# Merging the convolution branch last in layer 0 of a two-block network, with most of its taps behind attention

## The reference, cut to what matters

```python
def conv_module(val, glu, gate, dw_w, dw_b, ln_g, ln_b, w_o):
    u = val * jax.nn.sigmoid(glu)
    u = lax.conv_general_dilated(u, dw_w[:, None, :], ..., feature_group_count=D_CONV) + dw_b   # 31 taps
    u = jax.nn.silu(layer_norm_2(u, ln_g, ln_b)) * jax.nn.silu(gate)
    return u @ w_o
...
def merge(p, ya, yb, yc):
    return (sigmoid(p[13]) * ya + sigmoid(p[14]) * yb + sigmoid(p[15]) * yc) @ w_out
xs = xs + gate_x * merge(px, ya_x, yb_x, yc_x)
if need_ctx:                    # layer 0 only
    cs = cs + gate_c * merge(pc, ya_c, yb_c, yc_c)
```

## Time and profile before

| | us |
|---|---|
| median of 3 executions | 1399.64 (1398.94 to 1400.97) |
| profiled execution, own time | 1403.85 |
| its span, first to last instruction | 1402.5 |
| TensorE busy in the span | 1318.3 (94%) |
| VectorE, ScalarE, GpSimd busy | 865.4, 594.3, 278.2 |
| mean granted TensorE clock, share of full | 0.964 |

### The profile page before, as it was taken

One profiled execution on the slowest core, in us unless ns is written; L12 is line 12 of the kernel. 1 busy time (PEld: TensorE's weight loads), 2 busy tenths in 40 slices (PEclk: granted clock), 3 DMA queues, 4 the chain that ended last, 5 costly groups with the idle time before them and its releaser, 6 DMA issues.

```text
span 1402.5 us, 18894 instructions
## 1 busy us (share of the span) xinstructions
PE 1318.3 (94%) x7490; PEld 1041.7 (74%) x7490; DVE 865.4 (62%) x1484; ACT 594.3 (42%) x983; POOL 278.2 (20%) x217
## 2 busy tenths in 40 slices
PE   7999887989979899997999999999999998799998
PEld 5777776867767777775777877777888876578876
DVE  4694646784578643488997532324586678845553
ACT  3444442444474455222434532223463563346442
POOL 0200102210022322237100011311252142201112
PEclk9999988999989999998999999999999998989998
DMA  7571566275253411111111122222553333123451
GB/s 250 213 256 57 181 224 210 91 254 182 91 181 111 158 61 52 55 61 61 62 59 45 61 90 90 91 90 90 156 175 95 106 106 93 57 77 121 147 177 66
DMA packets 49192, 168.46 MB, mean 120 GB/s; under 512 B 5862, under 2 KB 7078, under 8 KB 48848
## 3 DMA queue, kind: packets, MB, share of 16 engines
q1 hardware_dynamic: 49104, 167.26, 35.9%
HBM read 166.19 MB, written 1.05 MB: 119 GB/s over the span
## 4 chain that ended last, share of the span: by engine, by line
PE 72%; DVE 11%; issue 11%; POOL 4%; ACT 1%; DMA 1%; SPq 0%; POOLq 0%; DVEq 0%; ACTq 0%
PE bank L1467 15%; PE bank L1468 15%; PE bank L1469 15%; PE bank L1386 4%; PE bank L1780 3%; PE bank L1485 3%; DVE conv_val L2523 3%; DVE w_lo L2210 2%; PE bank L1486 2%; PE bank L1487 2%; PE bank L1755 1%; PE bank L1547 1%; PE bank L1510 1%; PE bank L1716 1%; PE bank L1463 1%
## 5 line engine op out<-in xcount | busy, mean ns | idle before, releaser
L1467 PE MATMUL bank<-w_hi,x_hi 128*128 128x512 f32 (+4 forms) x1120 | 466.0, 416 | 13.2 <-DVE w_lo L2210 8.0
L2210 DVE TENSOR_TENSOR w_lo<-w_raw,w_hi 128x1024 fp32r<-128x1024 f32 (+3 forms) x264 | 320.6, 1218 | 252.1 <-ACT w_hi L1817 251.8
L1817 ACT ACTIVATE w_hi<-w_raw 128x1024 fp32r<-128x1024 f32 (+3 forms) x264 | 270.1, 1027 | 439.3 <-PE bank L1469 263.4
L1468 PE MATMUL bank<-w_lo,x_hi 128*128 128x512 f32 (+4 forms) x1120 | 437.7, 391 | 0.0
L1469 PE MATMUL bank<-w_hi,x_lo 128*128 128x512 f32 (+4 forms) x1120 | 437.3, 390 | 0.0
L1467 PEld LDWEIGHTS bank<-w_hi,x_hi 128*128 128x128 f32 x1120 | 216.4, 193 | 65.0 <-DVE w_lo L2210 11.4
L1469 PEld LDWEIGHTS bank<-w_hi,x_lo 128*128 128x128 f32 x1120 | 214.6, 192 | 46.9
L1468 PEld LDWEIGHTS bank<-w_lo,x_hi 128*128 128x128 f32 x1120 | 215.7, 193 | 39.4
L2523 DVE SCALAR_TENSOR_TENSOR conv_val<-conv_u,par,conv_val 128x512 f32<-128x512 f32 (+1 forms) x240 | 150.3, 675 | 0.0
L2843 POOL TENSOR_TENSOR merged<-merged,sigma 128x512 f32<-128x512 f32 x24 | 37.4, 1586 | 178.9 <-DVE sigma L2565 178.9
L1485 PE MATMUL bank<-x_hi,w_hi 128*128 128x512 f32 (+1 forms) x192 | 68.0, 354 | 0.5 <-ACT conv_val L2020 0.5
(11 more groups left out here) (331 smaller groups left out, 1759.0 us busy)
## 6 DMA issues: line engine op xcount, KB each, us to landing
w_raw<-in_w SPq DMA_DIRECT2D x172, 512.0 KB, 3.5
w_raw<-in_wm SPq DMA_DIRECT2D x48, 512.0 KB, 5.0
w_raw<-in_wo SPq DMA_DIRECT2D x40, 512.0 KB, 3.5
w_raw<-in_wy_gla SPq DMA_DIRECT2D x8, 512.0 KB, 3.5
w_raw<-in_wy_conv SPq DMA_DIRECT2D x8, 512.0 KB, 3.5
w_raw<-in_wy_att SPq DMA_DIRECT2D x8, 512.0 KB, 3.6
w_raw<-in_w SPq DMA_DIRECT2D x8, 460.0 KB, 5.6
w_raw<-in_w SPq DMA_DIRECT2D x12, 288.0 KB, 2.8
```

What stands on the lines that cost most here:

```text
L1467: mm(out, xh[:, q, col], hi[:, kk, 0:w], start=q == 0 and not with_bias, stop=False)
L1468: mm(out, xh[:, q, col], lo[:, kk, 0:w], start=False, stop=False)
L1817: do(hi, raw, ACT.Copy).then_inc(sem["cut_hi"], 1)
L2210: v.tensor_tensor(lo, raw, hi.bitcast(F32), ALU.subtract).then_inc(sem["cut_lo"], 1)
```

## The change

Layer 0 of block 2 merges in the order GLA, attention, convolution: M1A, y1, M1B, y1, AG, M2A, y2, M2B, y2, M0A, CGATE, y0, M0B, y0. Its taps 8 to 30 (of 0 to 30) may start only behind `att_out2` of the last query tile. In both layers the gate projection CGATE stands behind M0A and not ahead of it; layer 1 keeps the order (1, 0, 2) and its taps are not held. What waited for the last branch by name (y2, M2B) now asks which branch is last; `conv_hi`, which in layer 0 writes the buffer that the other branches' operands use, waits for the branch before.

```diff
-BRANCHES = [(1, 0, 2), (1, 0, 2)]
+BRANCHES = [(1, 2, 0), (1, 0, 2)]
...
+def last_branch(layer):
+    return f"y{BRANCHES[layer][-1]}"
+
+def last_merge_chunk(layer):
+    return MERGE[BRANCHES[layer][-1]][1]
...
     for i in BRANCHES[l]:
         first, second = MERGE[i]
+        if i == 2 and not gates_kept(l, AG):
+            yield from inp(AG, tiles, gated)
+        yield from inp(first, tiles, sigma)
         if i == 0:
             yield from project_t(l, CGATE)
-        elif i == 2 and not gates_kept(l, AG):
-            yield from inp(AG, tiles, gated)
-        yield from inp(first, tiles, sigma)
         if i == BRANCHES[l][0] and gates_kept(l, AG):
             yield from inp(AG, tiles, gated)
...
-        "merged": [("acc_add", "y2", l, g, t), ("project", "in2", l, M2B, NP - 1, tiles_of(l)[-1])]}[source],
+        "merged": [("acc_add", last_branch(l), l, g, t), ("project", "in2", l, last_merge_chunk(l), NP - 1, tiles_of(l)[-1])]}[source],
...
-    "tap": lambda l, n, j: [("tap", l, n - 1, j), ("conv_u", l, j)],
+    "tap": lambda l, n, j: [("tap", l, n - 1, j), ("conv_u", l, j)] + tap_held(l, n),
...
+def tap_held(l, n):
+    at = BRANCHES[l].index(0)
+    return [("att_out2", l, tiles_of(l)[-1])] if at == 2 and n >= 8 else []
...
     def conv_hi(l, j):
         act.wait_ge("conv_g", l, j)
-        if l == 0:
-            act.wait_ge("project", "y1", l, 1, 1, 3)
-        else:
+        earlier = branch_before(l, 0)
+        if earlier is not None:
+            act.wait_ge("project", f"y{earlier}", l, 1, 1, tiles_of(l)[-1])
+        if l > 0:
             act.wait_ge("project", "in2", l, GV, NP - 1, 3)
```

More of the change, by code:

```diff
@@ L811 @@
         "y1": [("gated", l, GG, t)] + before_flip(l, 1), "y2": [("gated", l, AG, t)] + before_flip(l, 2),
-        "merged": [("acc_add", "y2", l, g, t), ("project", "in2", l, M2B, NP - 1, tiles_of(l)[-1])]}[source],
+        "merged": [("acc_add", last_branch(l), l, g, t), ("project", "in2", l, last_merge_chunk(l), NP - 1, tiles_of(l)[-1])]}[source],
     "flip_hi": lambda source, l, t, g: [("flip", source, l, t, g)],
     "flip_lo": lambda source, l, t, g: [("flip_hi", source, l, t, g)],
-    "mi_sq": lambda l, t: [("out_add", l - 1, 1, t), ("acc_add", "y2", l - 1, 1, 3), ("mi_x", l - 1, 3)] + (
+    "mi_sq": lambda l, t: [("out_add", l - 1, 1, t), ("mi_x", l - 1, 3)] + ([("acc_add", last_branch(l - 1), l - 1, 1, 3)] if l > 0 else []) + (
         [("mi_sq", l, t - 2)] if l > 0 else [*BRANCHES_OVER, ("loads_context",)] if t in C_TILES else
@@ L859 @@
     "conv_g": lambda l, j: [("conv_silu", l, j), ("ev_cg", l, j)],
-    "conv_hi": lambda l, j: [("conv_g", l, j), ("project", "y1", l, 1, 1, 3) if l == 0 else ("project", "in2", l, GV, NP - 1, 3)],
+    "conv_hi": lambda l, j: [("conv_g", l, j)] + ([] if branch_before(l, 0) is None else [("project", f"y{branch_before(l, 0)}", l, 1, 1, tiles_of(l)[-1])]) + ([("project", "in2", l, GV, NP - 1, 3)] if l > 0 else []),
     "conv_lo": lambda l, j: [("conv_hi", l, j)],
@@ L1421, in flip @@
         elif source == "merged":
-            pe.wait_ge("acc_add", "y2", l, g, t)
+            pe.wait_ge("acc_add", last_branch(l), l, g, t)
         else:
@@ L1847, in flip_hi @@
         elif source == "merged":
-            act.wait_ge("project", "in2", l, M2B, NP - 1, tiles_of(l)[-1])
+            act.wait_ge("project", "in2", l, last_merge_chunk(l), NP - 1, tiles_of(l)[-1])
         high = b.y[l][0] if source in ("y1", "y2") else {"x1": m, "mix": m}.get(source, b).xh
@@ L1953, in mi_sq @@
             act.wait_ge("out_add", l - 1, 1, t)
-            act.wait_ge("acc_add", "y2", l - 1, 1, 3)
+            act.wait_ge("acc_add", last_branch(l - 1), l - 1, 1, 3)
             act.wait_ge("mi_x", l - 1, 3)
```

## The result

| | before | after |
|---|---|---|
| median | 1399.64 us | 1406.11 us (7 executions, 1404.17 to 1411.39) |
| profiled execution, own time and span | 1403.85, 1402.5 | 1406.71, 1405.4 |
| mean granted TensorE clock | 0.964 | 0.968 |

The ratio of after to before is 1.0043, 95% interval [1.0032, 1.0054]: the change makes the kernel slower by 0.43%, some 6.0 us. The prediction (1400.4, range 1393 to 1409) holds the time inside its range, but its sum of +0.8 us is wrong by 5 us and its likeliest case, "same", is not what happened. The time lies beside the 1406.5 of its rival "VectorE is late behind attention", whose wait did not occur, so that nearness is luck. The lines of the kernel after are numbered 14 or 15 higher.

The account below looks back on a forecast made before the run. TensorE, busy for 94% of the span, was taken as the bound, so only its stops and low clock could pay. Terms -5.7 - 2.5 + 1.5 + 3.5 + 2.5 + 1.5 = +0.8 on 1399.64 gave 1400.4 us, range 1393 to 1409.

Parts of the forecast that it names:

- same: Whole kernel: one stop exchanged for another, time within 0.2% (2.8 us), range 1397 to 1403; chance 0.42.
- VectorE is late behind attention: Rival: behind attention TensorE waits 4 to 8 us at L1611 and the clock drops; +6.8, some 1406.5 us; chance 0.31.
- (1): Layer 0's `y1` transposes: without taps beside GpSimd's chain the stop shrinks, -5.7 us, and the clock stays up, -2.5.
- (2): Attention in layer 0 loses its taps, but TensorE is already busy throughout and stays covered by projections: 0.
- (3): Behind attention in layer 0: 92 taps run there and TensorE waits for the mean matmul; +1.5 us, bounds 0 and 8.
- (4): Layer 0's `y0`: TensorE stands behind the gate projection now directly in front, +3.5 us, and the clock costs +2.5.
- (5): Layer 1: M0A and gate projection change places, so `y0` starts late; +1.5 us, bounds 0 and 5.
- The chain is 4.2 us: Layer 1: time from the first `ev_cg` to the end of the second `conv_lo`, 4.2 us.
- part of that is filled by attention's last products: Layer 1: attention's last products fill part of the some 2 us by which `y0` would start late.
- the forecast's better case: `y1` transposes: `gated` keeps its place in GpSimd's order and the stop shrinks to about 0.4 us.
- a wait of the `y2` transposes: Layer 0, attention's transposes: a wait there was listed as a sign of a wrong prediction, with no size given.
- a full block: Behind attention: eight GpSimd instructions of 1.3 us block up to 10.4 us of taps; sum would end 5 us higher.

Follow-up runs that it names:

- e1: Kernel after with the gate projection ahead of M0A again in layer 1 alone; 1402.86 us, ratio to the kernel before 1.0012.
- e3: Kernel after without the hold of the taps, new branch order and moved gate projection kept; 1405.53 us, ratio to the kernel before 1.0029.
- e5: Kernel after with gate projection ahead of M0A in both layers and layer 0's taps from 14 on held behind the last `gated(AG)`; 1396.37 us, ratio 0.9966.
- e8: Kernel after, gate projection ahead of M0A in both layers, taps from 5 held behind attention's last output, from 12 behind its last `gated`; 1399.28 us, ratio 0.9982.
- e13: Kernel after, gate projection ahead of M0A, taps from 14 behind last `gated(AG)`, GpSimd's first and last `gated(GG)` ahead of query tiles three and four; 1394.96 us, 0.9965.
- e4: Kernel before with only the gate projection moved behind M0A in both layers; 1414.12 us, ratio to the kernel before 1.0093.
- e6: Kernel before, old orders kept, with layer 0's taps 8 to 30 waiting for the last `gated(GG)`; 1395.20 us, ratio 0.9955.
- e10: Kernel before, layer 0's taps 8 to 30 behind the last `gated(GG)`, first and last `gated(GG)` ahead of query tiles three and four on GpSimd; 1388.81 us, 0.9908.
- e2: Kernel after with the gate projection ahead of M0A again in both layers; 1401.08 us, ratio to the kernel before 0.9999.

## Why the prediction was right and wrong, by its own terms

| part | forecast | measured in the profiled pair |
|---|---|---|
| (1) stop at the `y1` transposes, clock behind it | -5.7 - 2.5 | -3.2 - 1.0 |
| (2) attention, AG, M2A, `y2` transposes | 0 | +3.1 + 1.7 |
| (3) wait for the mean | +1.5 | 0 |
| (4) `y0` in layer 0, clock | +3.5 + 2.5 | +1.65 + 0 |
| (5) layer 1 | +1.5 | +4.2 + 1.7 |
| sum | +0.8 | +8.2 |

Terms (5) and (2) failed, and the gain of (1) was taken too large. The shift from one stop to others was forecast in kind; where they lie and what they cost was not.

**Part (5) is the mis-sized term**: the mechanism (a bare chain from the gate's evacuation to `y0`) was named, its bounds 0 to 5 nearly held the 5.9, and the value was taken low. It held no term for the clock, which cost 1.7. Two steps of its working failed. "The chain is 4.2 us" was read where no other work lay between its steps, and moved to a place where `gated` and a weight cut fell into it: 6.4 us. And "part of that is filled by attention's last products" was wrong: they stood ahead of the last gate matmuls, so nothing filled it. e1 shows that this term is most of the loss: 4.3 of the 6.0 us.

**Part (1)** had the cause right: e3 brings the 7.9 us back by the taps alone. The gain was 4 us short of the forecast. By its own numbers 7.93 less 7.0 leaves a stop of 0.9 us and not 0.4.

GpSimd's timeline of the kernel after, answering to the earlier trace rows:

```profile
645.73 2.20 POOL L2939 TENSOR_TENSOR att_q<-gate_tmp 128x512 f32<-128x512 f32 x1 [2.34 <-DVE gate_tmp L2689]
648.08 1.04 POOL L2924 TENSOR_TENSOR gate_tmp<-att_q 128x512 f32<-128x512 f32 x1
650.12 1.65 POOL L2930 TENSOR_TENSOR att_ms<-att_ms,minus_half 128x8 f32<-128x8 f32 x1 [1.00 <-DVE att_ms L2668]
651.74 1.29 POOL L2933 TENSOR_TENSOR att_q<-att_q,rows 128x512 f32<-128x512 f32 x1
...
653.99 1.71 POOL L2864 TENSOR_TENSOR gla_v<-gla_v,merged 128x512 f32<-128x512 f32 x1
657.66 2.54 POOL L2930 TENSOR_TENSOR att_ms<-att_ms,minus_half 128x8 f32<-128x8 f32 x1 [1.96 <-DVE att_ms L2668]
```

The third tile's pair fell to 2.94 us (forecast 2.8); `hr_add` stayed at 2.20 (forecast 1.3), with a weight cut of VectorE beside it (645.57, 1.22 us) in place of a tap; `gated` started at 653.99 (forecast 652.9), and as TensorE came 0.9 us earlier in this execution (652.81 against 653.73), that is 2.0 us late and not 1.1. It did keep its place ahead of the fourth pair, so even the forecast's better case was 2 us too good. The fourth pair came behind the first `gated`. It started only at 657.66, since its mean square (`hr_ms`) stood on VectorE behind a weight cut of 2.28 us, and it made a second stop of 2.28 us in front of the query heads' transposes, which the 7.9 us had hidden. That a shorter stop would leave the clock up did not hold: 2.94 us were followed by 3.05 us at 0.50.

**Part (2)** put the `y2` transposes at nothing, though "a wait of the `y2` transposes" was named among the signs of a wrong prediction. Four `gated` steps were counted in part (3) as neighbours of 92 taps with slack, and not as neighbours of the few taps in front of a `y_lo` that TensorE wants at once. With the two kept apart (e5) the stop and its stretch are gone.

**Part (3)**: the rival with 0.31 did not happen in the kernel after; the last tap started at 868.2 and was done at 868.9, ahead of TensorE's mean matmul at 869.9. Attention ended at 777.4, earlier than the 793 "at the latest", and that was its reserve. e8 (1.24 us) and e13 (1.88 us) show how thin it was.

**Part (4)**: the stop is 1.65 us and left the clock alone. The 3.5 rested on a third of a merged row: of the three `conv_lo` from 814.29 the first took 1.77 us by itself, beside `conv_g`, and ended at 816.1 and not at 815.3, which makes the forecast 4.2. In the kernel before the same swap costs 4.70 us, near that and near the upper bound of 5, and 2.2 for the clock, near the 2.5 that was taken (e4). By the timelines the place of the second `conv_hi` makes the difference; no run tests that alone, and the prediction had no term for it.

The measured sum of +8.2 is above the ratio's 6.0: single stretches at 0.50 differ between executions. In e4, where the terms are large, rows and ratio agree within 0.2 us.

## What to carry to other kernels

When work is moved to clear a crowded stretch, look at what lies beside it in the new place with the same eyes: here the gain was in keeping taps away from GpSimd's steps. One line that does only that (e6) wins 6.3 us, with the queue's order set right as well (e10) 12.9, where the reordering lost 6. A chain's length holds for the queue in which it was read; before it is laid bare, count every step of other work that each of its engines may place inside it. And where two causes make one wait, the worth of removing both is not the sum of each alone (here 0 and 6.3 us against 12.9): test them together too.

## What the hardware showed beside that

Taps and GpSimd's full-width steps that run side by side come near to taking turns. With `gated` beside them, four of the six taps after 797 took 1.77 us each, where a tap by itself takes 0.74; the four `gated` took 6.99 us in all, 1.75 each, where three of the same steps with no tap beside them took 1.29 each (e5, the row at 793.37). From one start to the next a tap and a `gated` took 1.70 us together; alone the taps follow each other every 0.66 us and the `gated` every 1.25, so full turns would make 1.91.

VectorE's six taps of the kernel after, and the 40 of the kernel before from 606 to 660, durations min/median/max in ns:

```profile
L2538 DVE SCALAR_TENSOR_TENSOR conv_val<-conv_u,par,conv_val x6: 745/1766/1778, 797.0 to 803.4; 128x512 f32<-128x512 f32 x6
L2523 DVE SCALAR_TENSOR_TENSOR conv_val<-conv_u,par,conv_val x40: 737/743/1786, 607.2 to 655.9; 128x512 f32<-128x512 f32 x40
```

The prediction had held a full block to be too dear, on the strength of a mean over those 40 taps. Taken one by one, 34 of them took 0.74 or 0.75 us and six took 1.52 to 1.79, and these six are the 5.5 us. Each of the six began while a 128x512 step of GpSimd was under way. Of the 34, ten ran beside GpSimd's power on 4 or 8 columns and were not longer for it, and six began just ahead of a 128x512 step. So the mean hid what one costs. The page "SBUF — State Buffer" of the Trainium skill (Who interferes with whom) calls the port pair that the two engines share an exclusive lock. The trace agrees in the main, with 1.70 us for a pair where full turns would make 1.91; the prediction had applied that rule to the wait for the mean, where slack took it up, and not to the `y2` transposes, where it cost 4.8 us.

Of the granted clock: in the kernel after, stops of 2.28 and 1.65 us were followed by no stretch at 0.50, stops of 2.94, 3.08 and 4.22 us by 3.0 to 3.4 us at that level. The length of a stop alone does not decide it: the stop of 1.84 us at layer 0's end is followed by no such stretch in the kernels before and after and by one of 6.8 us in e2. At the same stop of 4.50 us near 1163 the stretch was 10.2 us in the execution of before, 1.3 of it inside the stop, and 6.8 in that of after. A sum can carry such a term only with both ends.
